# Sparse attention: the convolution's banded weights are built by VectorE within the input projection instead of by GpSimd within the attention

## The reference, cut to what matters

```
proj = rms_norm(x) @ w_in                  # q, k and v of three branches, gates, u
attn_out = nsa_attention(q, k_cmp, v_cmp, k_slc, v_slc, k_win, v_win, gates)
a, g = split(u, 2);  h = a * sigmoid(g)    # 512 channels
y = depthwise_conv(pad(h), conv_w, taps=31) + conv_b
conv_out = silu(layer_norm(y, ln_g, ln_b))
x = x + concat(attn_out, conv_out) @ w_out
x = x + swiglu(h)   (layer 0)   or   x + moe_swiglu(h)   (layer 1)
```

## Time and profile before

| what | value |
|---|---|
| time, median of 3 runs | 2428.24 us (2427.86 to 2430.18) |
| span of the profiled execution, first to last instruction | 2425.3 us |
| difference of the median and the span | 2.94 us |
| busy share of the span: PE, DVE, ACT, POOL | 98%, 71%, 60%, 4% |
| mean granted TensorE clock | 0.990 |

### The profile page before, as it was taken

The page is one execution under the profiler, slowest core; times in us unless marked ns, Lnnn a source line. Parts: engine busy times, 40 slices in busy tenths (PEclk is TensorE's granted clock), DMA queues, the critical chain, the costliest instruction groups (busy, mean ns, idle before and its releaser), DMA issues.

```text
span 2425.3 us, 32059 instructions
## 1 busy us (share of the span) xinstructions
PE 2375.5 (98%) x12122; PEld 1950.6 (80%) x12122; DVE 1730.3 (71%) x2103; ACT 1447.4 (60%) x1761; POOL 85.7 (4%) x87
## 2 busy tenths in 40 slices
PE   9899999899999999999999999999999999999998
PEld 8578888667888888888888888888878888887887
DVE  7665446758988888898888898767455565755555
ACT  6544444547777777777777777665544446554443
POOL 1100000201000000000000000001000000000000
PEclk9999999989999999999999999999999999999999
DMA  7435555327999999999999999715535542453551
GB/s 261 159 127 188 191 190 159 121 93 256 360 352 366 347 372 350 368 349 369 347 370 344 373 348 371 242 54 184 182 122 190 182 149 87 158 190 105 191 191 44
DMA packets 249705, 569.99 MB, mean 235 GB/s; under 512 B 9664, under 2 KB 20352, under 8 KB 249600
## 3 DMA queue, kind: packets, MB, share of 16 engines
q1 hardware_dynamic: 249456, 568.30, 66.6%
q10 hardware_dynamic: 144, 0.26, 0.0%
HBM read 562.82 MB, written 1.05 MB: 232 GB/s over the span
## 4 chain that ended last, share of the span: by engine, by line
PE 93%; DVE 4%; ACT 2%; issue 1%; POOLq 0%; POOL 0%; ACTq 0%; DVEq 0%
PE PS L922 26%; PE PS L924 26%; PE PS L923 26%; PE PS L1075 2%; PE PS L1087 1%; PE PS L1545 1%; PE PS L1130 1%; PE PS L1374 1%; PE PS L994 1%; PE PS L1194 1%; PE PS L1113 1%; ACT SM L1817 1%; PE PS L1019 1%; PE PS L1335 1%; PE PS L983 1%
## 5 line engine op out<-in xcount | busy, mean ns | idle before, releaser
L2656 DVE TENSOR_TENSOR Wl<-ring,Wh 128x2048 fp32r<-128x2048 f32 x334 | 761.8, 2298 | 101.0 <-ACT Wh L1963 101.0
L1963 ACT ACTIVATE Wh<-ring 128x2048 fp32r<-128x2048 f32 x334 | 639.9, 1919 | 127.7 <-PE PS L924 127.7
L2227 DVE TENSOR_TENSOR Wl<-ring,Wh 128x2048 fp32r<-128x2048 f32 (+2 forms) x192 | 431.3, 2251 | 283.4 <-ACT Wh L1724 282.9
L1724 ACT ACTIVATE Wh<-ring 128x2048 fp32r<-128x2048 f32 (+2 forms) x192 | 361.5, 1890 | 237.5 <-PE PS L924 236.7
L922 PE MATMUL PS<-Wh,HTh 128*128 128x512 f32 (+3 forms) x1184 | 465.6, 393 | 4.2 <-DVE Wl L2227 2.4
L924 PE MATMUL PS<-Wh,HTl 128*128 128x512 f32 (+3 forms) x1184 | 457.5, 386 | 0.0
L923 PE MATMUL PS<-Wl,HTh 128*128 128x512 f32 (+3 forms) x1184 | 456.6, 386 | 0.0
L922 PE MATMUL PS<-Wh,xgh 128*128 128x512 f32 x896 | 354.6, 396 | 1.8 <-DVE Wl L2656 1.2
L924 PE MATMUL PS<-Wh,xgl 128*128 128x512 f32 x896 | 349.8, 390 | 0.0
L923 PE MATMUL PS<-Wl,xgh 128*128 128x512 f32 x896 | 349.2, 390 | 0.0
L922 PEld LDWEIGHTS PS<-Wh,HTh 128*128 128x128 f32 x1184 | 223.6, 189 | 50.2 <-issue 4.2
(11 more groups left out here) (346 smaller groups left out, 2469.3 us busy)
## 6 DMA issues: line engine op xcount, KB each, us to landing
ring<-in_moe_w_gate SPq DMA_DIRECT2D x112, 1024.0 KB, 7.1
ring<-in_moe_w_up SPq DMA_DIRECT2D x112, 1024.0 KB, 7.6
ring<-in_moe_w_down SPq DMA_DIRECT2D x112, 1024.0 KB, 7.1
ring<-in_mlp_w SPq DMA_DIRECT2D x64, 1024.0 KB, 5.3
ring<-in_w_in SPq DMA_DIRECT2D x27, 1024.0 KB, 5.2
ring<-in_w_out SPq DMA_DIRECT2D x16, 1024.0 KB, 6.9
ring<-in_cross_wkv SPq DMA_DIRECT2D x16, 1024.0 KB, 12.3
ring<-in_ffn_w_gate SPq DMA_DIRECT2D x14, 1024.0 KB, 5.1
```

What stands on the lines that cost most here:

```text
L1724: act.activation(Wh[:, i % SPLITS, 0:n], ring[:, r % RING, 0:n], ACT.Copy).then_inc(w_hi, 1)
L1963: act.activation(Wh[:, (base + i) % SPLITS, :], ring[:, (raw + i) % RING, :], ACT.Copy).then_inc(e_hi, 1)
L2227: dve.tensor_tensor(Wl[:, i % SPLITS, 0:n], ring[:, r % RING, 0:n], Wh[:, i % SPLITS, 0:n].bitcast(F32), ALU.subtract).then_inc(w_lo, 1)
L2656: dve.tensor_tensor(Wl[:, (base + i) % SPLITS, :], ring[:, (raw + i) % RING, :], Wh[:, (base + i) % SPLITS, :].bitcast(F32), ALU.subtract) ...
```

## The change

`conv_w` is written by VectorE with the same four products a layer: one between the split of piece 8 and the wait for the keys' power, three between the splits of pieces 10 and 11. Its home moves, two channel groups each, to `H` and to a part of `scr` (columns 1536 to 3583), so nothing waits for the projection to have released `HTh` and `HTl`. GpSimd's products and its waits on `taps_out` and on the projection go, and so does the wait of VectorE before it reuses `rt8`. PE's matmuls, their order and their waits stay the same but for where they read.

```diff
--- before.py
+++ after.py
@@ -125,7 +125,6 @@
         Wl = sb("Wl", [P, SPLITS, PIECE], F32R)
         X = sb("X", [P, T, D])
         H = sb("H", [P, T, D])
-        ht_at = nc.sbuf_base
         HTh = sb("HTh", [P, KC, S], F32R)
         HTl = sb("HTl", [P, KC, S], F32R)
         proj_at = nc.sbuf_base
@@ -136,7 +135,6 @@
         def over_scr(name, first, shape):
             return nc.alloc_sbuf_tensor_at(name, shape, F32R, offset=scr_at + 4 * first)
 
-        conv_w = nc.alloc_sbuf_tensor_at("conv_w", [P, CC, GROUPS * QUADS, ROWS], F32, offset=ht_at)
         sm_at = nc.sbuf_base
         SM = sb("SM", [P, 2, 4, S])
         PT = sb("PT", [P, 2, 2, 4, P])
@@ -194,6 +192,8 @@
 
         hid_rows_sb = otmp[:, 0:CMP_HID]
         QT = scr[:, 0:24 * S].rearrange("p (m s) -> p m s", s=S)
+        conv_w = [home.rearrange("p (n j q r) -> p n (j q) r", n=2, j=GROUPS, q=QUADS)[:, n]
+                  for home in (H[:].rearrange("p t d -> p (t d)"), scr[:, 6 * S:6 * S + 2 * GROUPS * QUADS * ROWS]) for n in range(2)]
         CT = scr[:, 4096:4096 + CC * CT_W].rearrange("p (c s) -> p c s", c=CC)
         Y = scr[:, 5248:5248 + CC * S].rearrange("p (c s) -> p c s", c=CC)
         SQ = scr[:, 4096:4096 + CC * S].rearrange("p (c s) -> p c s", c=CC)
@@ -827,14 +827,6 @@
                     pool.tensor_tensor(row_rs[:, slot, :], mean_sq[:, slot, :], mhalf[:].to_broadcast([P, T]),
                                        ALU.pow).then_inc(rs_out, 1)
 
-            def conv_weights(layer, chunks):
-
-                for ch in chunks:
-                    taps = tap_rows[:, layer, ch].rearrange("p j q -> p (j q)")
-                    pool.tensor_tensor(conv_w[:, ch, :, :], taps.unsqueeze(2).to_broadcast([P, GROUPS * QUADS, ROWS]),
-                                       row_mask[:].unsqueeze(1).to_broadcast([P, GROUPS * QUADS, ROWS]),
-                                       ALU.mult).then_inc(conv_w_ok, 1)
-
             n = 0
             for tile, v in ((ones, 1.0), (ident, 0.0)):
                 pool.memset(tile[:], v).then_inc(pool_seq, 1)
@@ -871,10 +863,7 @@
             for layer in range(LAYERS):
                 row_power(0)
                 power(T * HEADS, T * 2 * KV_HEADS)
-                pool.wait_ge(taps_out, 1)
                 power(2)
-                pool.wait_ge(lin_full, layer * LIN1 + 12)
-                conv_weights(layer, CONV_ORDER)
                 power(T)
                 row_power(0)
             pool.memset(dispT[:].bitcast(F32), 0.0).then_inc(zeroed, 1)
@@ -1542,7 +1531,7 @@
                     moving = shifted(layer, ch)
                     for q in range(part * QUADS // 2, (part + 1) * QUADS // 2):
                         for j in range(GROUPS):
-                            mm = pe.matmul(PS[ROWS * j:ROWS * (j + 1), 6, 0:S], conv_w[:, ch, j * QUADS + q, :],
+                            mm = pe.matmul(PS[ROWS * j:ROWS * (j + 1), 6, 0:S], conv_w[ch][:, j * QUADS + q, :],
                                            moving[:, j, SHIFTS * q:SHIFTS * q + S], start=(q == 0), stop=(q == QUADS - 1))
                     if part == 1:
                         mm.then_inc(conv_full, 1)
@@ -2883,6 +2872,14 @@
                     dve.tensor_tensor(x1, parts[0], parts[1], ALU.subtract)
                     return dve.tensor_tensor(x2, parts[2], parts[3], ALU.add)
 
+                def conv_weights(chunks):
+
+                    for ch in chunks:
+                        taps = tap_rows[:, layer, ch].rearrange("p j q -> p (j q)")
+                        dve.tensor_tensor(conv_w[ch], taps.unsqueeze(2).to_broadcast([P, GROUPS * QUADS, ROWS]),
+                                          row_mask[:].unsqueeze(1).to_broadcast([P, GROUPS * QUADS, ROWS]),
+                                          ALU.mult).then_inc(conv_w_ok, 1)
+
                 dve.wait_ge(lin_out, base + 2)
                 head_squares(0, HEADS)
                 if layer == 0:
@@ -2900,6 +2897,7 @@
                 head_squares(HEADS, 2 * KV_HEADS)
                 c.piece += 1
                 ahead()
+                conv_weights(CONV_ORDER[0:1])
                 power()
                 head_scale(HEADS, 2 * KV_HEADS)
                 head_gain(HEADS, KV_HEADS, 2)
@@ -2909,7 +2907,10 @@
                 ahead()
                 if layer == 1:
                     distances()
-                c.piece += 2
+                c.piece += 1
+                ahead()
+                conv_weights(CONV_ORDER[1:])
+                c.piece += 1
                 ahead()
                 kk = kc_sb[0:NCMP, 0:2, :]
                 c.lin = base + 9
@@ -2954,7 +2955,6 @@
                     elif i == 8:
                         mix_low(0)
                     elif i == 9 and layer == 1:
-                        dve.wait_ge(conv_w_ok, LAYERS * CC)
                         dve.tensor_tensor(both_halves, ident[0:16, 0:8], ident[0:16, 8:16], ALU.add)
                         dve.memset(rt8[:, 2:4, 0:8], 0.0)
                     elif i == 10:
```

## The result

The changed kernel took 2402.36 us (median of 4 runs, 2401.76 to 2411.37) against 2428.05 us before; the ratio is 0.9904, with a 95% interval of 0.9887 to 0.9922. The ratio is the time over that of the kernel before. The forecast was 2416 us, range 2412.5 to 2421: the way was right, the gain twice what was said. The profiled execution has a span of 2400.0 us against 2425.3, and a mean granted clock of 0.998 against 0.990.

A forecast was written before the change was run, and what follows sets the result against it. PE was taken as the bound (93%), with VectorE alone setting the end from the second `glu` to unit 1's transposes. 5.8 + 5.8 - 0.7 + 1.2 = 12.1 us off 2428.24 gave 2416 us, range 2412.5 to 2421.

The forecast's parts named there:

- What the change removes: From `glu` to unit 1's transposes, four VectorE instructions slowed by GpSimd's `conv_w` products get shorter: 5.8 us a layer.
- PE follows, and the transfers follow: Unit 1's transposes start at 76.4 to 76.7 us, loss 0 to 0.3; convolution transfers land 0.2 to 1.6 us early.
- 6 to 7 us named as a sign: The stretch from `glu` to the first convolution matmul would be shorter by this much in each layer.
- What the change adds: Eight VectorE products in the projection at 1.23 us each: hidden in layer 0, 0.7 us reach the chain in layer 1.
- GpSimd's power against the first product: In the projection, the first product runs beside the power at no cost; rival that it waits: 2417.6 us, 10%.
- The clock: After the removed waits PE's clock recovers: 1.2 us, both layers, ends 0 and 3; no recovery or late transfers 14%.
- The sum: Over both layers, 5.8 + 5.8 - 0.7 + 1.2 = 12.1 us off 2428.24, said as 2416 us.
- The row of 494 to 498 us: Granted clock 0.63 though PE worked 2.97 of 4 us, so the clock's gain was called no certainty.
- The range: Whole kernel: 2412.5 us (full clock return in both layers, products hidden) to 2421 us (dear products).

The follow-up runs named there:

- experiment 3: Changed kernel, but GpSimd makes the four products, in the projection right after the keys' power, VectorE's taken out: 2414.48 us, ratio 0.9949.
- experiment 9: Kernel before, with 6, 6, 2 and 3 unread matmuls in PE's waits before units 0, 1, 7 and 10: 2413.14 us, ratio 0.9945.
- experiment 7: Changed kernel, with 1, 2 and 3 unread matmuls in PE's waits before units 1, 7 and 10: 2401.48 us, ratio 0.9891.
- experiment 11: Changed kernel, with 3 unread matmuls in PE's wait before unit 10 only: 2401.97 us, ratio 0.9897.
- experiment 2: Changed kernel, with VectorE stalled by 4 idle products, about 2.9 us, at each of two places a layer: 2426.93 us, ratio 0.9991.
- experiment 4: Change in layer 0 alone; in layer 1 GpSimd makes the products at the old time, in the new homes: 2419.82 us, ratio 0.9959.

## Why the prediction was wrong, by its own steps

- **What the change removes**: 5.8 us a layer was said, 5.93 and 5.95 came, and 11.7 us for both with the clock held. Right. That GpSimd is the cause is shown by experiment 3, where other VectorE instructions are held instead.
- **PE follows, and the transfers follow**: PE took the transposes as VectorE released them. SP's transfers began at 73.64 us, 3.67 after `glu`, and PE reached the convolution at 79.36 with no wait for them. Right. From `glu` to there the change took off 7.06 us in layer 0 and 7.53 in layer 1, a little more than the 6 to 7 us named as a sign.
- **What the change adds**: eight products of 1.22 us, hidden in layer 0. In layer 1 I had 0.7 us on the chain; the stretch before `glu` grew by 0.18. Back-to-back products start 1.14 us apart, not 1.23, and some of the covers were longer than the idle times I had added up.
- **GpSimd's power against the first product**: no hold. The power of 8 values took 3.61 us as before, the product beside it 1.22. The rule of the Trainium skill ("SBUF — State Buffer", Who interferes with whom), an exclusive lock for the whole instruction, fits the 128x1024 products on GpSimd and not this 8-value power. Where the two differ the measurement decides.
- **The clock**: this step failed. It was priced at 1.2 us, with ends 0 and 3, and is 12.8 us in the two traces and 14.2 us by experiment 9. The sum took only the low stretches next to the removed waits and let the clock there be half a chance. It priced neither the second low stretch at the end of each attention, where PE ran the layer norm's small matmuls, the last units and the first matmuls of `w_out` at the lower level, nor that this stretch can vanish. The row of 494 to 498 us was read as a reason for doubt, where it was part of the price: it lies right behind unit 7's wait in layer 1, and behind the same wait, at 475.5 us, the changed kernel's clock was 1.00.
- **The range** followed from that: its lower end allowed for 3 us of clock. No rival had the clock as more than a few microseconds on the good side. With the terms as the traces have them the sum is 11.9 - 0.2 + 12.8 = 24.5 us: 2428.24 - 24.5 = 2403.7.

What stays open: why the late fall came, as far as their times and clocks tell, in nearly all runs of the kernel before and in about half of those of the change. The changed kernel waits there for the same 1.52 us; experiments 7 and 11 show that this wait is needed for the long fall, not what decides in one execution. By luck of four runs the first result showed the change at its best: over both its batches its ten runs have a median of 2405.8 us, which is still below the range.

## What to carry to other kernels

Where a wait of the bounding engine goes, price its clock over everything behind it, not over the wait: list every stretch of low granted clock in the stage before making the sum. To separate delay from clock, fill PE's waits with matmuls nobody reads, in the kernel before and in the one after; the difference of the two is the delay, and the fill itself may be the cheapest gain of all. A profile is one execution: when runs of one kernel step by 4 to 5 us, compare the clocks of several before a single trace is explained.

## What the runs showed of the hardware

- Unread matmuls in waits of 2.9, 1.23 and 1.52 us, some 17 of 0.45 us a layer, made the kernel before faster by 14.2 us.
- An extra 128x256 float32 matmul took 0.45 us, so 10 of them overfilled a wait of 2.9 us.
- A GpSimd product of 128x1024 with two SBUF inputs held one two-input VectorE instruction each, however small (15x128 or 128x4). A GpSimd power held none: the 128x1120 split beside the one of 16 values took 1.32 us, the 128x1024 product beside the one of 8 took 1.22.
- PE waits of 1.52 us let the clock fall to the lower level in some executions and not in others, and so did waits of 1.23 us in the kernel before (0.63 behind one, 1.00 behind the other). Unfilled waits of 2.9 to 3.5 us did in every trace that has them, those of the kernel before and of experiments 2, 3 and 4.
